# Another order of the work behind the norms, and a pre-norm vector multiplied into the weights' split

## What is computed

```
x = x + 0.5 * rms_norm(swiglu(rms_norm(x, g_ffn1_pre), wg, wu, wd), g_ffn1_post)
mixed = hybrid_mixer(rms_norm(x, g_mix_pre), w_in, ..., w_out, ...)
x = x + rms_norm(mixed, g_mix_post)
x = x + 0.5 * rms_norm(swiglu(rms_norm(x, g_ffn2_pre), wg, wu, wd), g_ffn2_post)

swiglu(x, wg, wu, wd) = (silu(x @ wg) * (x @ wu)) @ wd
rms_norm(x, gain)     = x * rsqrt(mean(x * x, axis=-1) + 1e-6) * gain
```

## Time and profile before

| | us |
|---|---|
| median of 3 runs | 2248.50 |
| lowest and highest run | 2247.97, 2252.68 |
| the profiled execution's own time | 2248.52 |
| its span | 2246.7 |
| TensorE busy | 2152.1 |
| VectorE busy | 1211.5 |
| ScalarE busy | 984.1 |
| GpSimd busy | 325.5 |

### The profile page before, as it was taken

How to read it: one execution, slowest core, us unless ns; L and a number is a source line. 1 busy time by engine, 2 the same in 40 slices (tenths; PEclk the granted TensorE clock), 3 DMA queues, 4 the chain that set the end, 5 groups by cost and what they waited for, 6 DMA issues and landing times.

```text
span 2246.7 us, 31714 instructions
## 1 busy us (share of the span) xinstructions
PE 2152.1 (96%) x13641; PEld 1933.8 (86%) x13641; DVE 1211.5 (54%) x1159; ACT 984.1 (44%) x1048; POOL 325.5 (14%) x186
## 2 busy tenths in 40 slices
PE   6969999999999999998999999999998999999998
PEld 5739999998999998887998987887887998897887
DVE  5535454663554554545565665446554565576553
ACT  4324343334353444444345555435444334556443
POOL 2102430223334300001120021001000130021000
PEclk9859999999999999998999999999999999999999
DMA  6104545642455546553533345555554452344553
GB/s 191 66 0 160 178 168 177 203 156 76 138 177 172 169 168 204 188 174 127 178 122 112 111 153 172 189 183 169 187 176 162 150 169 94 113 151 151 187 187 112
DMA packets 219435, 343.77 MB, mean 153 GB/s; under 512 B 5706, under 2 KB 152300, under 8 KB 219196
## 3 DMA queue, kind: packets, MB, share of 16 engines
q1 hardware_dynamic: 218684, 339.70, 45.6%
q10 hardware_dynamic: 272, 1.65, 0.2%
q0 software_dynamic: 368, 0.79, 0.2%
HBM read 341.07 MB, written 1.05 MB: 152 GB/s over the span
## 4 chain that ended last, share of the span: by engine, by line
PE 86%; DVE 5%; ACT 4%; DMA 2%; POOL 1%; issue 1%; SPq 0%; DVEq 0%; POOLq 0%
PE banks L309 15%; PE banks L311 14%; PE banks L310 14%; PE banks L460 10%; PE banks L463 10%; PE banks L461 10%; PE banks L1511 3%; PE banks L1053 2%; PE banks L1287 2%; ACT w_hi L295 1%; DVE w_lo L302 1%; DVE hT L684 1%; PE banks L499 1%; DVE xn_lo L670 1%; DMA raw<-ffn_wg 1%
## 5 line engine op out<-in xcount | busy, mean ns | idle before, releaser
L302 DVE TENSOR_TENSOR w_lo<-raw,w_hi 128x2048 fp32r<-128x2048 f32 x321 | 757.5, 2362 | 521.7 <-ACT w_hi L295 521.4
L295 ACT ACTIVATE w_hi<-raw 128x2048 fp32r<-128x2048 f32 x321 | 613.1, 1913 | 768.4 <-DMA raw<-w_in 153.1
L309 PE MATMUL banks<-xn_hi,w_hi 128*128 128x272 f32 (+1 forms) x2224 | 654.0, 294 | 13.2 <-DVE y L1686 6.2
L311 PE MATMUL banks<-xn_hi,w_lo 128*128 128x272 f32 (+1 forms) x2224 | 645.3, 290 | 0.0
L310 PE MATMUL banks<-xn_lo,w_hi 128*128 128x272 f32 (+1 forms) x2224 | 644.2, 290 | 0.0
L309 PEld LDWEIGHTS banks<-xn_hi,w_hi 128*128 128x128 f32 x2224 | 431.6, 194 | 19.4 <-DVE y L1686 7.0
L310 PEld LDWEIGHTS banks<-xn_lo,w_hi 128*128 128x128 f32 x2224 | 431.9, 194 | 0.4
L311 PEld LDWEIGHTS banks<-xn_hi,w_lo 128*128 128x128 f32 x2224 | 430.9, 194 | 0.0
L460 PE MATMUL banks<-w_hi,xn_hi 128*128 128x512 f32 x768 | 304.5, 396 | 3.9 <-DVE y L1793 1.8
L461 PE MATMUL banks<-w_lo,xn_hi 128*128 128x512 f32 x768 | 300.9, 392 | 0.0
L463 PE MATMUL banks<-w_hi,xn_lo 128*128 128x512 f32 x768 | 296.1, 392 | 0.0
(11 more groups left out here) (304 smaller groups left out, 2532.5 us busy)
## 6 DMA issues: line engine op xcount, KB each, us to landing
raw<-w_in SPq DMA_DIRECT2D x60, 1024.0 KB, 5.1
raw<-ffn_w_gu SPq DMA_DIRECT2D x44, 1024.0 KB, 5.1
raw<-ffn_wd SPq DMA_DIRECT2D x44, 1024.0 KB, 4.9
raw<-ffn_wg SPq DMA_DIRECT2D x40, 1024.0 KB, 5.1
raw<-ffn_wu SPq DMA_DIRECT2D x40, 1024.0 KB, 5.1
raw<-ret_w_in SPq DMA_DIRECT2D x24, 1024.0 KB, 5.2
raw<-ffn_w_down SPq DMA_DIRECT2D x22, 1024.0 KB, 4.9
raw<-ret_w_out SPq DMA_DIRECT2D x8, 1024.0 KB, 5.0
```

Source lines behind the costliest of these rows:

```text
L295: nc.scalar.activation(w_hi[:, n0 % SLOTS, :], raw[:, n0 % SLOTS, :], ACT.Copy).then_inc(S["w_hi"], 1)
L302: nc.vector.tensor_tensor(w_lo[:, n0 % SLOTS, :], raw[:, n0 % SLOTS, :], w_hi[:, n0 % SLOTS, :].bitcast(F32), ALU.subtract).then_inc(S["w_ ...
L309: e.matmul(out, wh, xh, start=start, stop=False)
L311: return e.matmul(out, wl, xh, start=False, stop=stop)
```

## The change

The change has four parts.

1. **The order in `act_post` and `dve_post`**, for all six posts. The scaling of `tb` = 1 (square, root, reciprocal, write to `ysb`) moves ahead: on ScalarE behind the fills of tiles 0 to 3 of `tb` = 0, on VectorE behind the add of tile 4 of `tb` = 0. ScalarE squares `hT` for both halves only at the very end.
2. **The pre-norm's gain** of the feed-forwards 3, 4 and 5 goes into the weights: a split of their 66 gate and up chunks is four instructions of 512 columns with a gain column (`GAINED`) in place of one of 2048. In posts 1, 2 and 4 `xn_hi` and `xn_lo` are then written without a gain, four tiles by one instruction (`tok4`, `hcol4`).
3. **The split of chunk `base + 2`** of these three feed-forwards moves into the post, between the fills of the two halves (`ahead`).
4. **TensorE** computes chunk `base + 2` for `tb` = 0 before it begins with `tb` = 1 of chunk `base`.

```diff
+GAINED = {BASE[f"gu{_f}"] + _c: (_g, 4 * (_c % 2)) for _f, _g in ((3, 64), (4, 8), (5, 72)) for _c in range(NGU)}
...
         def split_hi(n0, i):
...
+            if isinstance(i, int) and n0 in GAINED:
+                g = G2 + sum(GAINED[n0])
+                for x in range(4):
+                    c = slice(x * 512, x * 512 + 512)
+                    ins = nc.scalar.activation(w_hi[:, n0 % SLOTS, c], raw[:, n0 % SLOTS, c], ACT.Copy, scale=gcol[:, g + x:g + x + 1])
+                ins.then_inc(S["w_hi"], 1)
+                return
...
         def split_lo(n0, i):
...
+            if isinstance(i, int) and n0 in GAINED:
+                g = G2 + sum(GAINED[n0])
+                for x in range(4):
+                    c = slice(x * 512, x * 512 + 512)
+                    ins = nc.vector.scalar_tensor_tensor(out=w_lo[:, n0 % SLOTS, c], in0=raw[:, n0 % SLOTS, c],
+                                                         scalar=gcol[:, g + x:g + x + 1], in1=w_hi[:, n0 % SLOTS, c].bitcast(F32),
+                                                         op0=ALU.mult, op1=ALU.subtract)
+                ins.then_inc(S["w_lo"], 1)
+                return
...
-            for q in range(2):
-                last = quarter(base + q, 0, q, 0, True)
-                if q:
-                    last.then_inc(S["gmm"], 1)
-                if q == 0 and f > 2:
-                    pe_turn(j, 1, 6)
+            quarter(base, 0, 0, 0, True)
+            if f > 2:
+                pe_turn(j, 1, 6)
+            quarter(base + 1, 0, 1, 0, True).then_inc(S["gmm"], 1)
+            if f > 2:
+                quarter(base + 2, 1, 0, 0, False)
             for q in range(2):
                 quarter(base + q, 0, q, 1, True).then_inc(S["pe_chunk"], 1)
             for u in range(1, 11):
...
+                        if f > 2 and (u, q, tb) == (1, 0, 0):
+                            continue
...
             for c in range(2 * 11 + NDN):
-                split_hi(base + c + AHEAD, 0)
+                if c or f == 2:
+                    split_hi(base + c + AHEAD, 0)
...
-        def act_post(j, banks, g0):
...
+        def act_post(j, banks, g0, ahead=None):
...
+            def fill_hi(kt, tb):
                 if g0 is None:
...
+                    return
+                if ahead:
+                    if kt % 4 == 3:
+                        act.wait_ge(S["h2"], 16 * j + 8 * tb + kt + 1)
+                        act.activation(tok4(xn_hi, kt - 3, tb), hcol4(kt - 3, tb), ACT.Copy).then_inc(S["x2h"], 4)
+                    return
...
+            scale(0)
+            leave(0)
+            for kt in range(4):
+                fill_hi(kt, 0)
+            scale(1)
+            fill_hi(4, 0)
+            leave(1)
+            for kt in range(5, KT):
+                fill_hi(kt, 0)
+            if ahead:
+                split_hi(ahead, 0)
+            for kt in range(KT):
+                fill_hi(kt, 1)
+            if g0 is not None:
+                for tb in range(2):
+                    for half in range(2):
+                        act.activation(sq4[:, tb, half * 512:(half + 1) * 512].rearrange("p (n t) -> p n t", t=P),
+                                       hT[:, 4 * half:4 * half + 4, META + tb * P:META + tb * P + P], ACT.Square).then_inc(S["sq2"], 1)
...
+            leave(0)
+            for kt in range(KT):
+                add(kt, 0)
+                if kt:
+                    fill_lo(kt - 1, 0)
+                if kt == 4:
+                    leave(1)
+            fill_lo(KT - 1, 0)
+            if ahead:
+                split_lo(ahead, 0)
+            for kt in range(KT):
+                add(kt, 1)
+                if kt:
+                    fill_lo(kt - 1, 1)
+            fill_lo(KT - 1, 1)
```

More of the change, by code:

```diff
@@ L645, in dve_xffn, with scale @@
                     hidden_lo((9, 13, 17, 21, 23, 24).index(c))
-        def act_post(j, banks, g0):
-            for tb in range(2):
+        def act_post(j, banks, g0, ahead=None):
+            def scale(tb):
                 a = banks[tb] * 512
@@ L662, in act_post @@
-                for half in range(2):
-                    act.activation(sq4[:, tb, half * 512:(half + 1) * 512].rearrange("p (n t) -> p n t", t=P),
-                                   hT[:, 4 * half:4 * half + 4, META + tb * P:META + tb * P + P], ACT.Square).then_inc(S["sq2"], 1)
-        def dve_post(j, banks, turned, gy, g0):
-            def fill_lo(kt, tb):
-                dve.wait_ge(S["x2h"], 16 * j + 8 * tb + kt + 1)
-                dve.scalar_tensor_tensor(out=tok(xn_lo, kt, tb), in0=hcol(kt, tb), scalar=gcol[:, g0 + kt:g0 + kt + 1],
-                                         in1=tok(xn_hi, kt, tb).bitcast(F32), op0=ALU.mult, op1=ALU.subtract).then_inc(S["x2l"], 1)
-            for tb in range(2):
+                    return
@@ L679, in dve_post @@
                 dve.wait_ge(S["yrs"], 2 * j + tb + 1)
-                dve.tensor_scalar(ysb[:, tb, 512:1024], y, yrstd[:, tb:tb + 1], None, ALU.mult).then_inc(S["yvd"], 1)
-                for kt in range(KT):
-                    dve.wait_ge(S["yT"], 4 * j + 2 * tb + kt // 4 + 1)
-                    b = turned[2 * tb + kt // 4] * 512 + (kt % 4) * P
-                    dve.scalar_tensor_tensor(out=hcol(kt, tb), in0=ps[:, b:b + P], scalar=gcol[:, gy + kt:gy + kt + 1], in1=hcol(kt, tb),
-                                             op0=ALU.mult, op1=ALU.add).then_inc(S["h2"], 1)
-                    if kt and g0 is not None:
-                        fill_lo(kt - 1, tb)
@@ L688, in dve_post, with add @@
-                if g0 is not None:
-                    fill_lo(KT - 1, tb)
+                dve.tensor_scalar(ysb[:, tb, 512:1024], ps[:, a:a + 512], yrstd[:, tb:tb + 1], None, ALU.mult).then_inc(S["yvd"], 1)
+            def add(kt, tb):
+                dve.wait_ge(S["yT"], 4 * j + 2 * tb + kt // 4 + 1)
+                b = turned[2 * tb + kt // 4] * 512 + (kt % 4) * P
+                dve.scalar_tensor_tensor(out=hcol(kt, tb), in0=ps[:, b:b + P], scalar=gcol[:, gy + kt:gy + kt + 1], in1=hcol(kt, tb),
+                                         op0=ALU.mult, op1=ALU.add).then_inc(S["h2"], 1)
```

38 lines of the change are left out of this document (28 added, 10 removed).

## The result

The changed kernel takes 2260.81 us (median of 5, 2258.48 to 2261.84) where the kernel before takes 2249.77 us beside it (median of 5, 2247.97 to 2252.68). The ratio is 1.0052, with a 95% interval of [1.0039, 1.0065]: slower by 11.0 us, where 3.0 were forecast, and outside the range.

A forecast was written before the change was run, and what follows sets the result against it. TensorE is busy 2152.1 of 2246.7 us, so only idle time and lower-clock time can be won. +0.7 (posts 1, 2, 4), -0.6 (0, 3), +0.05 (5), about 0, with cold stretches +3.0: 2251.5 us, range 2245.5 to 2256.0.

The forecast's parts named there:

- the long chain to the first transposes: Last split before posts 1, 2, 4 lengthens the first stall: +0.93 us in post 2, +0.50 in posts 1 and 4.
- cold stretch: First transposes to the next post's quarter with TensorE at 1.2 GHz, not 2.4, after a stall: costs 1.55 us.
- E: In a post, the time when TensorE's last product for `tb` = 1 before the second transposes ends.
- Forecast for the clock: Posts 1, 2, 4: lower clock behind some longer first stalls and the idle before chunk `base + 2`, together +3.0 us.
- All long stalls go cold: Rival, chance 0.28: clock falls at first stalls of posts 2, 4 and at E + 7.4 in three posts; +5.2 us, 2253.7.
- That term of 0.7: Lower clock behind the 1.6 us idle before chunk `base + 2`: 0.7 us, in one or two posts of three.
- E to the statistic: Posts 1, 2, 4: 26.45 us against 26.8 and 26.9; -0.35 us in post 2, -0.45 each in posts 1 and 4.
- Posts 0 and 3: Posts leading into mixers: third chunk waits for GpSimd's statistic, over 4 us for 3.08; gain 0.3 us each, -0.6 in all.
- The rival that the mixers keep their 1.35 us: Rival, chance 0.08: the mixers' third chunk doesn't wait for GpSimd, so 2.1 us less than forecast, 2249.4.
- Cheap instructions: Rival, chance 0.14: four small split instructions cost little more than one (+0.25 ScalarE, +0 VectorE); 2244.5 us.
- Early scaling without effect: Rival, chance 0.05 with late chunks: second transposes still wait 2.00 us in post 2; some +6 us over three posts.
- Late chunks in the stream: Rival, chance 0.05 with early scaling: the 66 splits reach TensorE, 0.9 us for each late chunk, over 2256.

The follow-up runs named there:

- The delay pair: 7 constant products behind the first transposes of posts 0 to 4, in the kernel before (2249.89 us) and in the changed kernel without part 2 (2254.18 us).
- the two `warm` runs: 7 constant products ahead of the first transposes of posts 0 to 4, in the changed kernel (2252.99 us) and in the kernel before (2250.29 us).
- `no_pool`: Changed kernel with GpSimd's first two sums cut to 8 columns, leaving most squares out of the statistic: 2252.67 us, ratio 1.0004.
- `order_warm`: Changed kernel without part 2, with 7 constant products ahead of the first transposes of posts 0 to 4: 2244.57 us, ratio 0.9985.
- `one_both`: Changed kernel with high and low part of the 66 splits each one instruction of 2048 columns with a single gain column: 2248.94 us, ratio 0.9995.

## Why the prediction was wrong

**Right.** What bounds the kernel, and the price of the long chain to the first transposes. The first stalls of posts 1, 2 and 4 were to be 3.4, 2.63 and 3.3 us, and are 3.37, 2.85 and 3.38. The split was to take 2.42 us on ScalarE and takes 2.55 or 2.56; on VectorE 2.72, and takes 2.74. Here the prediction weighed a table of the Trainium skill (VectorE: DVE Perf Modes, section on the TRN2 errata), by which as an estimate four take 2.38 us, against a row of PSUM operands. The trace decides for the row: 2.74 us, and 0.75 for a single piece where the table gives 0.594. The 66 splits don't reach TensorE in the chunk stream: from the statistic to the next post it is 162.02 us before and 162.00 after in the stretch behind post 1, and within 0.03 us behind the two others too.

**The step that failed: whose time a cold stretch is.** The prediction priced a cold stretch at 1.55 us, as measured, and then counted it alike in both orders, and only for posts 1, 2 and 4. It compared the start of the second transposes, E + 4.8 before with E + 3.45 now, but took E as given. (In post 1, where E was 1340.81 behind a cold stretch, they started at 1344.04 before, E + 3.2: E came later and the second transposes did not.) The same edit that took ScalarE's fills and squares out of the way of the second `ysb` made TensorE the engine that ends last between the first and second transposes. A cold stretch there was free before (8.66 to 8.68 us) and costs 1.6 us now, in five posts, not three. In posts 1, 2 and 4 the longer first stall came with it. In posts 0 and 3 the stall was hardly longer (2.21 and 2.14 us for 2.04), and in other kernels stalls of 1.97 to 2.26 us were followed by either level, so that all five were cold in this execution is partly chance. Forecast for the clock: +3.0 us. Shown: 5.6 by the table. The delay pair and the two `warm` runs rest on the same mechanism. The rival *All long stalls go cold* was right on the first stalls of posts 1, 2 and 4. It stopped at 2253.7, since it had nothing for posts 0 and 3 and took the stretch of post 1, cold before as well, for no loss. The stall before chunk `base + 2`, 1.35 us, brought no cold stretch in any of the three posts: in post 2 the products behind 1549.16 take 0.39 to 0.40 us again. That term of 0.7, in one or two posts of the forecast and in three of the rival, was not there.

The forecast was 8.0 us short. Of these, 2.6 are the clock, some 4.0 the way from E to the statistic, 0.9 posts 0 and 3 at a held clock (+0.3 for -0.6), and 0.25 the first stalls. So the clock is the mechanism that the forecast missed, and the terms of the next paragraph are the larger size.

**E to the statistic.** It was to be 26.45 us and is 27.8 in post 2 (1539.20 + 0.64 to 1567.62): with a forecast of less than before it is now more. Two terms were too small. The wait for chunk `base + 3` is 1.71 for 0.9: the low part beside GpSimd takes 4.24 us for 3.65. The sum had taken the slowing of one long instruction, 3.07 / 2.29, for that of four short ones, and theirs is 4.24 / 2.74. The waits for `xn_lo` and chunk `base + 2` are together 0.1 less than forecast. And each idle costs 0.17 us beyond its length, which the sum left out: by the timeline products follow each other at 0.23 us but last 0.40, and that overlap is lost where one waits, three times a post. Together 4 us over three posts.

**Posts 0 and 3.** GpSimd's part was right: the statistic hangs on it, and at a held clock both orders give the same (27.4 and 27.56). The rival that the mixers keep their 1.35 us falls. The form was wrong: it said that the wait at the third chunk would grow to over 4 us. The 3.08 us wait did not grow. It is a chain that starts behind the statistic (3.08 in `no_pool` too), and what grows is the wait for `sacc` ahead of it, 2.2 us for 1.2 at the held clock. The forecast of -0.6 left out the wait for `xn_lo` at the mixer's first chunk (3.0 us in two posts) and the cold stretches, and came out as +2.7 in the profiled execution.

**Beside these** the profiled execution of the changed kernel has 2.35 us more in the second mixer, at a lower clock there, and it is 13.3 us longer in its span where the medians are 11.0 apart.

**The other rivals.** Cheap instructions: no. Early scaling without effect: no, the 2.00 us wait is gone. Late chunks in the stream: no.

## What to carry to other kernels

Before you move work off a path, ask what else hid behind it. A wait that another engine sets absorbs what the waiting engine loses, here a cold stretch or 1.6 us of added products; once the wait is gone, the loss is on the path, and the gain of the new order and the price of the old slack come in one number. Where an engine's clock falls behind its stalls, try a few products on constants in the stall. The same fillers were worth 7.8 us in the changed kernel and nothing in the one before, and beside fillers an edit that had shown 2 us by the whole times showed 5 in the stretches that it touches. Compare stretches of the trace as well as whole times: here the clock in untouched parts moved a whole time by several us. And fold a vector into a step only if the number of instructions stays: here the multiplication cost next to nothing, and cutting 66 splits into four instructions each, on two engines, cost the kernel 7 to 8 us.

## What the runs showed of the hardware

- Four VectorE instructions of 512 columns beside GpSimd's sums take 4.24 us for 2.74 alone, one of 2048 columns 2.76 to 3.07 for 2.3. GpSimd's sum of 512 columns takes 1.76 us beside a short piece for 3.22 beside a long one, and ends 1.14 or 1.15 us after VectorE's instruction in both cases.
- Seven constant products in a first stall leave a stall of 0.2 to 1.2 us ahead of the transposes (`order_warm`), and behind it all five intervals stay at the higher clock. Without them first stalls of 1.86 to 2.81 us were followed by either level (1.86 in `one_both` by the lower, 2.81 in the kernel before by the higher), those of 2.91 to 3.47 us always by the lower one.
- A gain column costs VectorE 0.06 us on an instruction of 2048 columns (2.35 us for 2.29). On ScalarE it costs 0.09 us an instruction (2.01 us for 1.92).
- With the same instructions, a mixer's interior takes 280.5 us at a mean granted clock of 0.99, 284.4 at 0.97 and 287.7 at 0.96.
